# Four banks for scores, three for turned probabilities, and the mixings of a group begun in the third slot of a step

## The chip, the cores and the metric

The kernel runs on one core of one Trainium2 chip. Its metric is the device time of one launch in microseconds (us). TensorE (PE in the profile) multiplies and turns tiles into the eight banks of PSUM; VectorE (DVE), ScalarE (ACT) and GpSimd (POOL) do the rest; SyncE (SP) issues most DMAs.

## What is computed

One step of a two-layer network over 1024 latent tokens and 128 prompt tokens. Each layer normalises its input, multiplies it by one wide weight matrix, and feeds three branches (a Fourier mixing, a pooling and an attention with eight heads). The change touches the attention, which is in the reference

```python
def one(qblk):
    s = jnp.einsum('bqhd,bkhd->bhqk', qblk, k, preferred_element_type=jnp.float32) * scale
    p = jax.nn.softmax(s, axis=-1).astype(v.dtype)
    return jnp.einsum('bhqk,bkhd->bqhd', p, v)
```

with 8 heads, keys of 96 numbers and values of 64. The 1024 latent queries attend to 1024 latent keys and 128 cached ones; the 128 prompt queries attend to their own 128 keys.

## The kernel before

**Tiles.** The queries of a head are nine tiles of 128 rows. Tiles 0 to 7 are latent: their 1152 keys make three score parts of 384 columns. Tile 8 is the prompt: one part of 128 columns. Over the head's nine tiles that is 25 parts, and 200 in a layer.

**Stages of a tile.** TensorE computes a score part in three passes (`scores`, L1778, passes at L1607 to L1609) into a bank. VectorE takes its row maxima (L1450) and, after the last part, the negated maximum (L1456). ScalarE reads the bank once more and writes the exponentials to SBUF (`exps`, L832, with a short instruction that reads the accumulated row sum); that gives the score bank back. TensorE turns the 128-column blocks of the exponentials (`turn`, L1798) into another bank; with the last part it also turns the inverse row sum (L1802), for which it waits for VectorE (L1469, L1474). ScalarE copies the turned part out (`turned_high`, L848, and L855 for the sums), VectorE subtracts for the low half (L1463), which gives that bank back. Two tiles make a group; TensorE multiplies the nine key tiles of a group by the values (`mix`, two passes a key tile, L1823 and L1824) in one accumulation in the one bank of the mixed outputs. ScalarE lifts half of it (L867), VectorE adds (L1484), which gives the mixed bank back.

**Steps.** The engines each run the same loop over steps s, one per tile, with h, j = divmod(s, 9): h is the head, j the place in it. In step s TensorE turns tile s-1, scores tile s+1 and mixes a piece of a group; at the step's end it may compute a piece of the next head's queries or keys (`beside_pe`, L1736). ScalarE copies out the parts of tile s-1 alternately with the exponentials of tile s: the copy of part 0, the exponentials of part 0, and so on; a piece of the next head's queries stands between the exponentials of part 0 and the copy of part 1. The order in TensorE's step is a table:

```python
PE_STEP = (("turn", 0), ("score", 0), ("mix", 0), ("turn", 1), ("score", 1), ("mix", 1),
           ("turn", 2), ("score", 2), ("mix", 2))
```

`mix_slots` (L203) says which key tiles of which group stand in the three mix slots of a step. A group's mixing begins in a step with odd j (3, 5, 7, or 0 of the next head) and ends in the step after it.

**Banks.** `bank_plan` (L108) gives each kind of item a range of banks. The items of a kind use its banks in turn. Before it writes an item, TensorE waits in `pe_takes` (L417) until the item that had the bank before was read out: with five banks score part n waits for the exponentials of part n-5. Kind "attn" holds the turned parts and the pieces of the next head, in program order; "score" the score parts; "mixed" the mixings; "chan" six items of the Fourier branch just ahead of the attention.

Of the kernel before, what the change touches and what calls it, by code (L numbers as in the profile page):

```python
# [30 lines left out]
TT = TOK // P  # L31
# [4 lines left out]
HEADS = 8  # L36
# [71 lines left out]
def bank_plan():  # L108

    phases = []  # L110
    def add(layer, name, first, banks, count):
        phases.append(((layer, name), first, banks, count))
    add(0, "vec", 6, 1, 1)
    add(0, "mod", 0, 6, 16)
    add(0, "modt", 6, 1, 1)
    add(0, "norm", 6, 2, NCH * KF)
    for l in range(DEPTH):
        add(l, "tok", 0, 3, 2 * TT)
        add(l, "feat", 0, 6, 3 * len(FEAT_COLS))
        add(l, "turn", 0, 6, 14)  # L120
        add(l, "pool", 6, 2, 6)
        add(l, "val", 6, 2, KS)
        add(l, "seq", 6, 2, 12)
        add(l, "chan", 0, 6, 6)
        add(l, "attn", 6, 2, len(attention_items()))
        add(l, "score", 0, 5, HEADS * (3 * TT - 2))
        add(l, "mixed", 5, 1, HEADS * GROUPS)
        add(l, "gate", 0, 3, 3 * 3 * KF)
        add(l, "branch", 3, 3, 3 * 3 * KF)
        if l == 0:  # L130
            add(l, "later", 6, 2, later(GATE_ROWS)[0])
        add(l, "gbc", 6, 2, 4)
        if l == 0:
            add(l, "last", 6, 2, len(LATER) - later(GATE_ROWS)[0])
        add(l, "out", 0, 6, 3 * TT)
        if l + 1 < DEPTH:
            add(l + 1, "norm", 6, 2, NCH * KF)
    used = [0] * 8
    plan = {}
    for key, first, banks, count in phases:  # L140
        plan[key] = (first, banks, [used[first + i] for i in range(banks)])
        for i in range(banks):
            used[first + i] += len(range(i, count, banks))
    return plan
# [19 lines left out]
def later(u):  # L164

    units = 3 * KF - 2
    return range(len(LATER) * min(u, units) // units, len(LATER) * min(u + 1, units) // units)
# [9 lines left out]
GROUPS = 5  # L177
# [3 lines left out]
def parts(m):  # L181

    return 1 if m % TT == 8 else 3
# [19 lines left out]
def mix_slots(s):  # L203

    slots = [None, None, None]
    h, j = divmod(s, TT)
    if j in (3, 5, 7) and h < HEADS:
        slots[1], slots[2] = (h, (j - 3) // 2, (0, 1)), (h, (j - 3) // 2, (2, 3, 4))
    if j in (4, 6, 8) and h < HEADS:
        slots = [(h, (j - 4) // 2, (5,)), (h, (j - 4) // 2, (6, 7)), (h, (j - 4) // 2, (8,))]  # L210
    if h and j == 0:
        slots[1], slots[2] = (h - 1, 3, (0, 1)), (h - 1, 3, (2, 3, 4))
    if h and j == 1:
        slots = [(h - 1, 3, (5,)), (h - 1, 3, (6, 7)), (h - 1, 3, (8,))]
    if h and j == 2:
        slots[1] = (h - 1, 4, (0,))
    return slots


# [18 lines left out]
def mixed_in(s):  # L238

    for slot in mix_slots(s):  # L240
        if slot and (slot[2][-1] == 8 or slot[1] == 4):
            return slot[:2]
    return None


def beside(s):

    h, j = divmod(s, TT)
    if j in BESIDE_STEPS and h + 1 < HEADS:
        n = BESIDE_STEPS.index(j)  # L250
        return [("qk"[n // 3], h + 1, n % 3)]
    return []


def attention_items():

    order = [(kind, 0, i) for kind in "kq" for i in range(3)]
    for s in range(STEPS):
        if 1 <= s <= TILES:
            order += [("t", s - 1, g) for g in range(parts(s - 1))]  # L260
        order += beside(s)
    return {key: n for n, key in enumerate(order)}


def hybrid_step(nc, x_prompt, x_sample, cache_ckv, cache_krope, c, c_ctx, norm_g, w_mod, b_mod, w_in,
                pool_w, pool_scale, q_norm_g, w_q_up, kv_norm_g, w_kv_up, w_br_a, w_br_b, w_br_c,
                w_out, final_norm_g, tab, y_prompt, y_sample, new_ckv, new_krope, park_hi, park_lo, rows_mid):
    plan = bank_plan()


# [1331 lines left out]
    def _(pe):  # L1602
# [47 lines left out]
        for l in range(DEPTH):  # L1650
# [201 lines left out]
            for s in range(STEPS):  # L1852
                if s > TILES:
                    gate_high(s - TILES)
                for what, c in PE_STEP:
                    if s == TILES and (what, c) == ("mix", 1):
                        gate_high(0)
                    if what == "score" and s + 1 < TILES and c < parts(s + 1):
                        scores(s + 1, c)
                    if what == "turn" and turned(s - 1, c) is not None:  # L1860
                        turn(s - 1, turned(s - 1, c))
                    if what == "mix" and mix_slots(s)[c]:
                        mix(*mix_slots(s)[c])
                for it in beside(s):
                    beside_pe(*it)
# [88 lines left out]
```

## Time and profile before

| | us |
|---|---|
| median of 3 runs | 2224.97 |
| lowest and highest | 2221.03, 2226.98 |
| the profiled execution | 2222.64 |
| span of its trace | 2220.4 |
| the two attention loops in it | 304 to 621.4 and 1386 to 1703.5 |

The profiled execution took 2.2 us more than its span: that much lies around the first and the last instruction. A page row gives an engine's busy time and its share of the span. In the listing of waits a row says which engine and line waited for which, the total, the number of waits and the longest. In a timeline row stand the start, the duration, the engine, the line, the operation with output and input, and in brackets the idle time just ahead of it with what ended it.

### The profile page before, as it was taken

The page shows a single profiled execution, that of the slowest core. Times are in us where ns is not written, and L with a number is a line of the kernel's source. Part 1 is how long each engine was busy: PE and PEld are TensorE (multiplying, and loading weights), DVE is VectorE, ACT ScalarE, POOL GpSimd, SP SyncE. Part 2 cuts the span into 40 slices and gives each one's busy share as a digit, 9 for nine tenths or more (in the row PEclk, how much of TensorE's full clock was granted, in tenths as well). Part 3 has the DMA queues.
Part 4 walks back from the last instruction along what each step waited for, and adds up shares of the span by engine and source line. Part 5 has one row for each costly group of instructions (what it writes and reads, how often), then busy time and mean ns, then how long its engine had stood idle before and what let it go on. Part 6 is the DMA issues. An engine that isn't in the chain of part 4 may idle for free.

```text
span 2220.4 us, 35875 instructions
## 1 busy us (share of the span) xinstructions
PE 2131.5 (96%) x13185; PEld 2035.3 (92%) x13185; DVE 1090.4 (49%) x2823; ACT 886.7 (40%) x2223; POOL 653.6 (29%) x560
## 2 busy tenths in 40 slices
PE   7999999999999999999999999999999999999997
PEld 5899878888899999999989997888888999999997
DVE  2441268888864667663162314888886111120213
ACT  2521267777831212113152214777777112111312
POOL 1323122322322234333441311222323223343342
PEclk8999999999999999999999999999999999999999
DMA  9811000000343333224255100000005111111232
GB/s 275 267 33 31 26 1 1 1 1 1 121 155 85 95 83 100 78 63 143 74 197 163 40 1 26 1 2 1 1 14 192 48 36 48 40 46 39 65 124 85
DMA packets 194622, 155.67 MB, mean 70 GB/s; under 512 B 8637, under 2 KB 186001, under 8 KB 193425
## 3 DMA queue, kind: packets, MB, share of 16 engines
q1 hardware_dynamic: 194448, 153.38, 22.2%
q8 instruction: 106, 1.74, 0.3%
q14 instruction: 68, 0.55, 0.1%
HBM read 124.89 MB, written 28.48 MB: 69 GB/s over the span
## 4 chain that ended last, share of the span: by engine, by line
PE 84%; DVE 7%; ACT 4%; issue 3%; DMA 1%; POOL 0%; SPq 0%; DVEq 0%; POOLq 0%; ACTq 0%
PE ps L1607 23%; PE ps L1609 23%; PE ps L1608 23%; PE ps L1798 5%; PE ps L1823 3%; PE ps L1824 2%; DVE partmax L1450 1%; DVE probsT L1463 1%; PE ps L1617 1%; DVE kT L1420 1%; ACT kT L879 1%; PE ps L1841 1%; ACT probsT L848 1%; DVE xn_high L1201 1%; ACT probs L832 1%
## 5 line engine op out<-in xcount | busy, mean ns | idle before, releaser
L1607 PE MATMUL ps<-xn_high,split_br 128*128 128x384 f32 x1584 | 531.8, 336 | 0.0
L1609 PE MATMUL ps<-xn_high,split_br 128*128 128x384 f32 x1584 | 529.5, 334 | 0.0
L1608 PE MATMUL ps<-xn_low,split_br 128*128 128x384 f32 x1584 | 529.3, 334 | 0.0
L960 ACT ACTIVATE sigmoids<-ps 128x384 f32<-128x384 f32 x144 | 70.4, 492 | 613.5 <-PE ps L1609 613.5
L1608 PEld LDWEIGHTS ps<-xn_low,split_br 128*128 128x128 f32 x1584 | 297.5, 188 | 0.0
L1607 PEld LDWEIGHTS ps<-xn_high,split_br 128*128 128x128 f32 x1584 | 297.4, 188 | 0.0
L1609 PEld LDWEIGHTS ps<-xn_high,split_br 128*128 128x128 f32 x1584 | 297.3, 188 | 0.0
L1002 POOL TENSOR_TENSOR split_br<-raw,split_br 128x1024 fp32r<-128x1024 f32 x82 | 198.2, 2418 | 320.4 <-ACT split_br L693 320.4
L1463 DVE TENSOR_TENSOR probsT<-ps,probsT 128x384 fp32r<-128x384 f32 x384 | 213.1, 555 | 70.1 <-ACT sum_inv_rows L855 42.7
L832 ACT ACTIVATE probs<-ps,negmax 128x384 f32<-128x384 f32 (+1 forms) x400 | 229.1, 573 | 29.3 <-DVE negmax L1456 28.7
L1798 PE MATMUL ps<-ident,probs 128*128 128x128 f32 x1168 | 197.5, 276 | 31.0 <-DVE kT L1420 15.8
L848 ACT ACTIVATE probsT<-ps 128x384 fp32r<-128x384 f32 x384 | 188.6, 491 | 79.9 <-PE ps L1798 46.7
L1450 DVE TENSOR_REDUCE partmax<-ps 128x1 f32<-128x384 f32 (+1 forms) x400 | 212.1, 534 | 2.0 <-PE ps L1609 1.8
L1541 DVE TENSOR_TENSOR products<-ps,sigmoids 128x384 f32<-128x384 f32 x96 | 53.5, 557 | 293.0 <-PE ps L1609 240.3
L1798 PEld LDWEIGHTS ps<-ident,probs 128*128 128x128 f32 x1168 | 132.0, 140 | 70.6 <-issue 65.3
L1136 POOL TENSOR_TENSOR merged<-merged,products 128x384 f32<-128x384 f32 x90 | 92.2, 1025 | 334.7 <-DVE products L1541 333.8
L1607 PE MATMUL ps<-split_br,xn_high 128*128 128x256 f32 (+1 forms) x576 | 182.2, 316 | 5.3 <-DVE xn_low L1204 5.0
L1609 PE MATMUL ps<-split_br,xn_low 128*128 128x256 f32 (+1 forms) x576 | 178.7, 310 | 0.0
L1608 PE MATMUL ps<-split_br,xn_high 128*128 128x256 f32 (+1 forms) x576 | 178.7, 310 | 0.0
L1823 PE MATMUL ps<-probsT,head_values 128*128 128x256 f32 x576 | 156.3, 291 | 12.0 <-DVE mixed_out L1484 12.0
L1607 PE MATMUL ps<-kT,qT 128*128 128x384 f32 (+1 forms) x400 | 163.3, 408 | 1.6 <-ACT probs L832 1.0
L1091 POOL TENSOR_TENSOR branch<-mixed_out,branch 64x256 f32<-64x256 f32 (+1 forms) x80 | 54.2, 678 | 335.3 <-DVE mixed_out L1484 334.4
(227 smaller groups left out, 4197.4 us busy)
## 6 DMA issues: line engine op xcount, KB each, us to landing
raw<-in_w_in SPq DMA_DIRECT2D x74, 512.0 KB, 3.9
raw<-in_w_mod SPq DMA_DIRECT2D x48, 512.0 KB, 5.0
park_high<-xn_high SPq DMA_DIRECT2D x6, 1536.0 KB, 6.4
park_low<-xn_low SPq DMA_DIRECT2D x6, 1536.0 KB, 10.6
xn_high<-park_high SPq DMA_DIRECT2D x2, 4608.0 KB, 16.0
rows<-in_x_sample SPq DMA_DIRECT2D x16, 512.0 KB, 6.8
raw<-in_w_out SPq DMA_DIRECT2D x16, 512.0 KB, 6.5
rows_mid<-rows SPq DMA_DIRECT2D x9, 512.0 KB, 2.6
```

The lines of the kernel that those rows point to most:

```text
L832: a.activation((P0, P1)[m % 2][:, c * CH:c * CH + w], PS[:, b, 0:w], ACT.Exp, bias=negmax[:, m % 2:m % 2 + 1], accum_out=partsum[:, m % 2, ...
L848: ins = a.activation(turned_place(m, gg, 0), PS[:, b, 0:n * P].rearrange("p (k c) -> p k c", k=n), ACT.Copy)
L960: a.activation(sig[:, ch, :], PS[:, b, 0:CH], ACT.Sigmoid).then_inc(bank_free[b], 1)
L1002: g.tensor_tensor(d[:, 1], raw_unit(n), d[:, 0].bitcast(F32), ALU.subtract).then_inc(S("split_low"), 1)
L1136: g.tensor_tensor(Y[:, u % KF, sl], Y[:, u % KF, sl], prod[:, q % 2, :], ALU.add).then_inc(S("y_sum"), 1)
L1450: v.tensor_reduce(partmax[:, m % 2, c:c + 1], PS[:, b, 0:w], AX.X, ALU.max).then_inc(S("partmax"), 1)
L1463: v.tensor_tensor(turned_place(m, gg, 1), PS[:, b, 0:n * P].rearrange("p (k c) -> p k c", k=n), turned_place(m, gg, 0).bitcast(F32), ALU.s ...
L1607: mm(out, wh, xh, start=first, stop=False)
L1608: mm(out, wh, xl, start=False, stop=False)
L1609: return mm(out, wl, xh, start=False, stop=last)
L1798: ins = nc.tensor.transpose(PS[:, b, q * P:(q + 1) * P], (P0, P1)[m % 2][:, (3 * gg + q) * P:(3 * gg + q + 1) * P], ident[:])
L1823: mm(PS[:, b, 0:w], vhl, xh, start=(kt == 0 or gr == 4), stop=False)
```

## The change

The banks of the attention's kinds are cut otherwise: "score" has four banks in place of five (0 to 3), "mixed" moves from bank 5 to bank 4, "attn" has three in place of two (5 to 7), and "chan" loses its sixth bank. And where a group's mixing began with two key tiles in the second slot and went on with three in the third, it now begins with five in the third. The steps in which a mixing ends keep their slots (one, two and one key tiles). The prompt tile's mixing moves from the second slot of its step to the third.

```diff
-        add(l, "chan", 0, 6, 6)
-        add(l, "attn", 6, 2, len(attention_items()))
-        add(l, "score", 0, 5, HEADS * (3 * TT - 2))
-        add(l, "mixed", 5, 1, HEADS * GROUPS)
+        add(l, "chan", 0, 5, 6)
+        add(l, "attn", 5, 3, len(attention_items()))
+        add(l, "score", 0, 4, HEADS * (3 * TT - 2))
+        add(l, "mixed", 4, 1, HEADS * GROUPS)
...
     if j in (3, 5, 7) and h < HEADS:
-        slots[1], slots[2] = (h, (j - 3) // 2, (0, 1)), (h, (j - 3) // 2, (2, 3, 4))
+        slots[2] = (h, (j - 3) // 2, (0, 1, 2, 3, 4))
...
     if h and j == 0:
-        slots[1], slots[2] = (h - 1, 3, (0, 1)), (h - 1, 3, (2, 3, 4))
+        slots[2] = (h - 1, 3, (0, 1, 2, 3, 4))
...
     if h and j == 2:
-        slots[1] = (h - 1, 4, (0,))
+        slots[2] = (h - 1, 4, (0,))
```

The instructions of VectorE, ScalarE, GpSimd and SyncE keep their order. TensorE's change at two places; in the brackets stand the semaphores that an instruction waits for, and bank_free with a number means that this bank must have been read out.

The first place is TensorE from the second turned part of a step with odd j to the third score part (step j = 3 of head 0). Before:

```order
L1798 MATMUL ps<-ident,probs_94 128x128 x2
L1607 MATMUL ps<-kT,qT 128x384 [waits bank_free3]
L1608 MATMUL ps<-kT,qT 128x384
L1609 MATMUL ps<-kT,qT 128x384
L1823 MATMUL ps<-probsT,head_values 128x256 [waits bank_free6,v_ready,bank_free5]
L1824 MATMUL ps<-probsT,head_values 128x256
L1823 MATMUL ps<-probsT,head_values 128x256
L1824 MATMUL ps<-probsT,head_values 128x256
L1798 MATMUL ps<-ident,probs_94 128x128 [waits bank_free6,bank_free3]
L1798 MATMUL ps<-ident,probs_94 128x128 x2
L1802 MATMUL ps<-ident,sum_inv 128x128 [waits sum_inv]
L1607 MATMUL ps<-kT,qT 128x384 [waits bank_free4]
```

Of the change:

```order
L1798 MATMUL ps<-ident,probs_94 128x128 x2
L1607 MATMUL ps<-kT,qT 128x384 [waits bank_free1]
L1608 MATMUL ps<-kT,qT 128x384
L1609 MATMUL ps<-kT,qT 128x384
L1798 MATMUL ps<-ident,probs_94 128x128 [waits bank_free6,bank_free0]
L1798 MATMUL ps<-ident,probs_94 128x128 x2
L1802 MATMUL ps<-ident,sum_inv 128x128 [waits sum_inv]
L1607 MATMUL ps<-kT,qT 128x384 [waits bank_free2]
L1608 MATMUL ps<-kT,qT 128x384
L1609 MATMUL ps<-kT,qT 128x384
L1823 MATMUL ps<-probsT,head_values 128x256 [waits bank_free5,bank_free6,v_ready,bank_free4]
L1824 MATMUL ps<-probsT,head_values 128x256
```

The four matmuls of two key tiles no longer stand between the second score part and the third turned part.

The second place is TensorE where one head passes into the next (step j = 0), from its first score part on; that step has two score parts before its one turned part. Before:

```order
L1607 MATMUL ps<-kT,qT 128x384 [waits bank_free4]
L1608 MATMUL ps<-kT,qT 128x384
L1609 MATMUL ps<-kT,qT 128x384
L1823 MATMUL ps<-probsT,head_values 128x256 [waits bank_free7,bank_free6,bank_free5]
L1824 MATMUL ps<-probsT,head_values 128x256
L1823 MATMUL ps<-probsT,head_values 128x256
L1824 MATMUL ps<-probsT,head_values 128x256
L1798 MATMUL ps<-ident,probs_94 128x128 [waits bank_free6,bank_free4]
L1802 MATMUL ps<-ident,sum_inv 128x128 [waits sum_inv]
L1607 MATMUL ps<-kT,qT 128x384 [waits bank_free0]
```

Of the change:

```order
L1607 MATMUL ps<-kT,qT 128x384 [waits bank_free1]
L1608 MATMUL ps<-kT,qT 128x384
L1609 MATMUL ps<-kT,qT 128x384
L1798 MATMUL ps<-ident,probs_94 128x128 [waits bank_free5,bank_free0]
L1802 MATMUL ps<-ident,sum_inv 128x128 [waits sum_inv]
L1607 MATMUL ps<-kT,qT 128x384 [waits bank_free2]
L1608 MATMUL ps<-kT,qT 128x384
L1609 MATMUL ps<-kT,qT 128x384
L1823 MATMUL ps<-probsT,head_values 128x256 [waits bank_free5,bank_free4]
L1824 MATMUL ps<-probsT,head_values 128x256
```

The mixing, with its wait for the mixed bank, has moved behind the turned part and the third score part.

## Rows read from the trace of the kernel before

**Rows 1.** Page, part 1: busy time, share of the span, instructions.

```profile
PE 2131.5 (96%) x13185; PEld 2035.3 (92%) x13185; DVE 1090.4 (49%) x2823; ACT 886.7 (40%) x2223; POOL 653.6 (29%) x560
```

**Rows 2.** Windows of both attention loops: length, busy time by engine, PEclk, DMA share, GB/s.

```profile
304.00:621.40 317.40, 295.12 (x2014) 267.98 (x2013) 264.38 (x751) 252.12 (x758) 90.11 (x107) 1.00 0.08 28
1386.00:1703.50 317.50, 294.91 (x2012) 267.79 (x2011) 263.94 (x751) 251.78 (x758) 89.80 (x106) 1.00 0.08 28
```

**Rows 3.** Listing of waits of the whole trace, TensorE's in the attention.

```profile
PE ps L1798 <- DVE kT L1420: 15.8, 42, 0.5
...
PE ps L1798 <- DVE probsT L1463: 12.5, 34, 0.7
PE ps L1823 <- DVE mixed_out L1484: 12.0, 20, 0.7
```

**Rows 4.** Timeline, start of the first loop: an exponential, and TensorE waiting for it.

```profile
305.86 0.58 ACT L832 ACTIVATE probs<-ps,negmax 128x384 f32<-128x384 f32 x1 [0.19 <-DVE negmax L1456]
...
306.59 0.45 PE L1607 MATMUL ps<-kT,qT 128*128 128x384 f32 x1 [0.50 <-ACT probs L832]
```

**Rows 5.** Timeline of TensorE, step j = 3 of head 3 and the next step's first row.

```profile
437.30 0.52 PE L1798 MATMUL ps<-ident,probs 128*128 128x128 f32 x3
...
438.72 0.42 PE L1607 MATMUL ps<-kT,qT 128*128 128x384 f32 x1
...
440.16 0.42 PE L1607 MATMUL ps<-kT,qT 128*128 128x384 f32 x1
...
441.48 0.34 PE L1607 MATMUL ps<-qhatT,wq_head 128*128 128x384 f32 x1
...
442.53 0.27 PE L1798 MATMUL ps<-ident,probs 128*128 128x128 f32 x1
```

**Rows 6.** Timeline of ScalarE, the same step: exponentials of parts 0 and 1.

```profile
438.25 0.57 ACT L832 ACTIVATE probs<-ps,negmax 128x384 f32<-128x384 f32 x1
...
439.59 0.59 ACT L832 ACTIVATE probs<-ps,negmax 128x384 f32<-128x384 f32 x1
```

**Rows 7.** Timeline, step j = 4: exponentials of part 0, second score part, next step.

```profile
443.44 0.58 ACT L832 ACTIVATE probs<-ps,negmax 128x384 f32<-128x384 f32 x1
...
443.86 0.42 PE L1607 MATMUL ps<-kT,qT 128*128 128x384 f32 x1
...
447.05 0.52 PE L1798 MATMUL ps<-ident,probs 128*128 128x128 f32 x3
```

**Rows 8.** Timeline, steps j = 5 and 6 and the first row of j = 7.

```profile
448.45 0.57 ACT L832 ACTIVATE probs<-ps,negmax 128x384 f32<-128x384 f32 x1
...
452.30 0.49 PE L1798 MATMUL ps<-ident,probs 128*128 128x128 f32 x3
...
453.36 0.57 ACT L832 ACTIVATE probs<-ps,negmax 128x384 f32<-128x384 f32 x1
...
454.02 0.52 PE L1798 MATMUL ps<-ident,probs 128*128 128x128 f32 x3 [0.47 <-DVE kT L1420]
...
457.49 0.52 PE L1798 MATMUL ps<-ident,probs 128*128 128x128 f32 x3 [0.38 <-DVE probsT L1463]
```

**Rows 9.** Timeline, step j = 7: VectorE's inverse sum, its turning, the next step.

```profile
459.49 0.16 DVE L1474 RECIPROCAL sum_inv<-rowsum 128x1 f32<-128x1 f32 x1
...
459.89 0.27 PE L1802 MATMUL ps<-ident,sum_inv 128*128 128x128 f32 x1
...
460.71 0.49 PE L1798 MATMUL ps<-ident,probs 128*128 128x128 f32 x3
```

**Rows 10.** Timeline, from head 3 into head 4 (j = 0), up to j = 1.

```profile
465.51 0.33 PE L1607 MATMUL ps<-kT,qT 128*128 128x384 f32 x1
...
466.42 0.58 ACT L832 ACTIVATE probs<-ps,negmax 128x384 f32<-128x384 f32 x1 [0.86 <-DVE negmax L1456]
...
466.90 0.39 PE L1823 MATMUL ps<-probsT,head_values 128*128 128x256 f32 x1 [0.71 <-DVE mixed_out L1484]
...
468.94 0.49 PE L1798 MATMUL ps<-ident,probs 128*128 128x128 f32 x3
```

## The prediction, made before the result

> **What bounds the kernel now.** I read the page first: TensorE is busy for 96% of the span, VectorE for 49% [rows 1]. That is a mean over stages, so the windows of the two attention loops come next, since the change touches little else: of 317.4 and 317.5 us TensorE is busy for 295.1 and 294.9, VectorE for 264 and ScalarE for 252, at full clock [rows 2]. TensorE sets the pace there too, with 44.9 us without work. The listing of waits says what that is [rows 3]: 28.3 us ahead of turned parts (L1798), which wait for VectorE to empty an "attn" bank (15.8 and 12.5 us), and 12.0 us ahead of mixings, which wait for VectorE to empty the mixed bank. These 40.3 us are all that the change can remove.
>
> **What one wait for a score bank looks like.** It happens once in a loop before. At 305.86 the exponentials of part 0 of tile 0 begin, and TensorE, which waits for that bank, goes on at 306.59 [rows 4]. So a score part can be written from 0.73 us after the start of the exponentials that give its bank back. I use this E + 0.73 throughout; it is one case, the same in both loops.
>
> **What four banks ask for.** In step s TensorE scores tile s+1. With five banks its second part needs the exponentials of tile s-1's last part, done in the step before. With four, part n needs n-4: the second part needs the exponentials of part 0 of tile s, the third those of part 1 of tile s. ScalarE makes these in the same step, and its order is unchanged: the exponentials of part 0 stand behind the copy of the turned part 0 of the same step. They cannot start earlier than the step allows, so TensorE's own step start sets a floor under its second score part.
>
> Issue costs of TensorE by differences of rows: a piece of queries takes 1.05 (441.48 to 442.53); third score part and three key tiles take 1.32 (440.16 to 441.48); second score part, two key tiles and the turned part with its sum take 1.44 (438.72 to 440.16) [rows 5]. With 0.24 for a key tile that makes 0.61 for a score part and 0.36 for the turned part with its sum; one without is 0.25. A piece of keys is three passes, 0.70, and 0.35 for the short last one.
>
> **Step j = 3**, times from its start at 437.30. Exponentials of part 0 start at 0.95, of part 1 at 2.29 [rows 6]. Before, the second score part starts at 1.42, the third at 2.86, the step ends at 5.23 [rows 5]. With the change the second waits until 0.95 + 0.73 = 1.68. The turned part follows at 2.29 and ends at 2.65, but the third score part needs 2.29 + 0.73 = 3.02. It ends at 3.63, then five key tiles (1.18) and the queries (1.05): 5.86. The step becomes 0.63 longer. Of this 0.47 is the two key tiles that before stood where TensorE now waits: the move takes away the very work that would cover the wait.
>
> **Step j = 4.** Exponentials at 0.91, second score part at 1.33 before [rows 5, 7], at 1.64 after: +0.31. The third needs nothing more, since two key tiles still lie between. At the end the next turned part waited about 0.2 for its bank before (the step lasts 4.52, its work 4.33); three banks remove that. Net +0.11.
>
> **Step j = 5.** Exponentials at 1.40 before [rows 7, 8], late because ScalarE first copies the piece of keys; that piece ends 0.2 later against the step's start, so 1.59. Second score part at 2.32, turned part, third at about 3.37 (bank of part 1), five key tiles, keys: 5.87 against 5.25: +0.62, although the wait for the keys' bank is gone.
>
> **Step j = 6** gains. Before it lasts 5.19, with a wait for an attn bank ahead of the second turned part and one of 0.38 behind the step [rows 8]; its work alone is 3.98. The exponentials start at 1.06 [rows 8], so the second score part waits until 1.79 in place of 1.34: 4.43, or -0.76.
>
> **Step j = 7** has one short score part. Before, two key tiles stand ahead of the third turned part, whose sum (VectorE, ready at 459.65) is turned at 459.89; the step lasts 3.22 [rows 8, 9]. After, nothing stands there: TensorE is at the sum some 1.1 us after the start and waits for VectorE, whose chain comes only 0.2 earlier on the clock while the step starts 0.76 earlier; the sum is turned at about 2.8, then five key tiles: 4.06, +0.84.
>
> **Head to head (j = 8 and 0).** From 460.71 to the next j = 1 are 8.23 us [rows 9, 10]. The second score part of j = 0 starts at 465.51 before; with four banks it needs exponentials that start at 466.42 because VectorE's maximum is late. VectorE's chain is 0.3 us earlier against the step's start after the change, so the part starts at about 6.1 rather than 4.80; before, TensorE then idled up to 466.90 for the mixed bank [rows 10], a wait that vanishes. From 6.1: score 0.61, turned part 0.24, score 0.61, five key tiles 1.18: 8.75, +0.52.
>
> **Steps j = 1 and 2** have the patterns of 4 and 3. I take +0.30 for j = 1 (the 0.31 of j = 4; no bank wait behind it) and +0.60 for j = 2 (near the 0.63 of j = 3; its one small mixing moves too, but its third part waits longer).
>
> **Sum.** 0.30 + 0.60 + 0.63 + 0.11 + 0.62 - 0.76 + 0.84 + 0.52 = 2.86 us a head, 16 heads: 45.8. Head 0 has no early mixings and comes out lower, head 7 has no pieces of a next head to lean on and comes out higher; I let them cancel. Start of a loop: the second score part of tile 1 now waits for the first exponentials instead of the third, about +0.5, less 0.3 for the third piece of keys just ahead, which no longer waits for a bank: +0.4 for two layers. "chan" with five banks: its sixth item takes the bank of its first, read long before, 0. Total +46 us. Against the profiled execution, 2222.6, this is 2269; that execution lies 2.3 below the median, well inside the runs' own spread, and I leave the figure there: 2269.
>
> **Bounds.** Low end: if only the waits of second score parts count and the third parts find their banks, j = 2, 3 and 5 fall to some 0.3 each and j = 7 to 0.3: about 1.0 a head, +16, 2239. High end: the gain of step 6 does not come, because ScalarE and VectorE are the ones who are late by then (+12), and ScalarE's lag in j = 5 carries on (+0.5 a head, +8): 2289.
>
> **Rivals.**
>
> A, faster: the removed waits decide. If the exponentials come earlier once the third score part stands ahead of the mixing, because their maximum is ready sooner, the floor falls away and the 40.3 us of [rows 3] go: 2182. It decides where exponentials of part 0 start less than about 0.6 us after the step; in the rows they start at 0.91 to 1.40, behind the copy of the turned part, not behind the maximum. Against it also [rows 7]: in j = 4 nothing waited, and 1.33 is still short of 1.64.
>
> The Trainium skill, page "Perfetto Trace Analysis", section "Optimization Strategy", says that a gap repeating on the engine that should be saturated can mean that there is not enough PSUM for the next tile; it speaks for a third bank ahead of L1798 and would give this rival's 2182 if the bank came free of charge. The rows show such gaps [rows 3, 8], but the bank is taken from scores, whose margin is negative.
>
> B, no change: new waits equal old ones, as where ScalarE's idle time lets it pull ahead by half of what is asked. Per head 2.5 us of old waits would have to be met by 2.5 of new: 2219 to 2231.
>
> C, slower but milder, second parts alone: 2231 to 2248, as in the low bound.
>
> D, worse: over 2292. ScalarE and VectorE, late in one step, push the next one's start; all terms as computed and +1.5 a head on top: 2293.
>
> **How the numbers follow.** Forecast (2248 to 2292) 0.66, A 0.07, B 0.05, C 0.15, D 0.07. A measurement of this kernel can tell about 0.3% from no change. A is faster, B the same, the rest slower: 0.07, 0.05, 0.88. The range from 2238 to 2292 leaves out A, B, D and a part of C, together just under 0.2 with half of C inside.
>
> **What would show it.** In the trace after: the waits of L1798 for VectorE (28.3 us) and of L1823 for the mixed bank (12.0) nearly gone; in their place TensorE's L1607 in the attention waiting for ScalarE's L832, some 60 to 80 us in about 150 waits and more, and L1802 for L1474 in step j = 7; loops of about 340 us in place of 317.4; the time outside them unchanged. Step j = 3 near 5.9 us and step j = 6 near 4.4. I am wrong if L832 starts less than 0.9 after the step, if a bank is free sooner than 0.73 after that, or if the loops are no longer.

## The result: 46.6 us slower, and the profile after

| | before | after |
|---|---|---|
| median of the runs shown, us | 2223.46 (4 runs) | 2270.05 (4 runs) |
| lowest and highest | 2221.03, 2226.98 | 2268.28, 2271.30 |
| span of the profiled execution | 2220.4 | 2269.1 |

The ratio is 1.0209, with a 95% interval of 1.0196 to 1.0223. The forecast was 2269, and its range 2238 to 2292.

The page answers [rows 1] with the same instructions and a lower share for TensorE. The second row is its chain of work that ended last; before, TensorE had 84% of that chain, VectorE 7% and ScalarE 4%.

```profile
PE 2142.5 (94%) x13185; PEld 2041.6 (90%) x13185; DVE 1092.5 (48%) x2823; ACT 886.1 (39%) x2223; POOL 652.6 (29%) x560
...
PE 79%; ACT 9%; DVE 6%; issue 5%; DMA 1%; POOL 0%; SPq 0%; DVEq 0%; ACTq 0%; POOLq 0%
```

The windows of the two attention loops answer [rows 2]. They are cut here from the first score part to the end of the last mixing; cut in that way, the loops before last 318.2 and 318.7 us with TensorE busy for 296.0 and 296.1.

```profile
302.10:643.40 341.30, 301.78 (x2016) 271.99 (x2017) 265.40 (x752) 252.06 (x758) 90.48 (x107) 1.00 0.07 26
1410.60:1752.20 341.60, 301.88 (x2016) 271.97 (x2017) 265.21 (x752) 252.10 (x758) 90.45 (x107) 1.00 0.07 26
```

Each loop is 23 us longer: +23.1 and +22.9. VectorE and ScalarE do the same work in it. Between the loops the trace is 3.7 us longer, ahead of them 1.1 us shorter, and behind them the same. So the traces differ by 48.7 us, of which 46.0 lie where the prediction put them.

The listing of waits answers [rows 3], and the page's groups give the same lines with their releasers.

```profile
PEld ps L1607 <- ACT probs L832: 99.7, 144, 1.9
...
PE ps L1607 <- ACT probs L832: 60.3, 88, 1.6
...
PE ps L1802 <- DVE sum_inv L1474: 9.4, 16, 0.8
```

```profile
L1607 PE MATMUL ps<-kT,qT 128*128 128x384 f32 (+1 forms) x400 | 168.0, 420 | 65.9 <-ACT probs L832 60.3
...
L1798 PE MATMUL ps<-ident,probs 128*128 128x128 f32 x1168 | 192.9, 273 | 4.1 <-DVE kT L1420 4.1
```

The waits of the turned parts fell from 28.3 us to 4.1, and those for the mixed bank from 12.0 to nothing that the listing shows. In their place stand 60.3 us of score parts (L1607) that wait for exponentials (L832).

TensorE's idle time in the loops grew by 34.3 us (44.9 to 79.2) and the loops by 46.0. The other 11.7 us appear as busy time, 603.7 in place of 592.0 us, although the instructions are the same. The rows of matmuls overlap. A score pass has a row of 0.34 us, but the next one starts 0.17 or 0.18 later, and busy time counts the overlap once. Where TensorE then waits, the row is counted whole. A score pass that starts behind a wait has a longer row besides (440 ns on the mean, against 411 without a wait), so the mean of the first score pass is 420 ns, against 408 before. The Trainium skill ("Perfetto Trace Analysis", section "Identifying the Most-Contended Engine") says that the busy share of matmuls is no good measure of how close a kernel is to TensorE's peak, since pipelined instructions look smaller in a trace. This trace agrees, as these 11.7 us show. **Loss is read from the length of a step, not from idle time alone.**

Step j = 3 of head 3 starts at 445.61 and answers [rows 5] and [rows 6]. The rows are TensorE's and ScalarE's timelines in order of time.

```profile
445.61 0.49 PE L1798 MATMUL ps<-ident,probs 128*128 128x128 f32 x3
...
446.47 0.49 PE L1798 MATMUL ps<-ident,probs 128*128 128x128 f32 x3
...
446.52 0.57 ACT L832 ACTIVATE probs<-ps,negmax 128x384 f32<-128x384 f32 x1
...
447.24 0.44 PE L1607 MATMUL ps<-kT,qT 128*128 128x384 f32 x1 [0.28 <-ACT probs L832]
...
447.86 0.59 ACT L832 ACTIVATE probs<-ps,negmax 128x384 f32<-128x384 f32 x1
...
448.20 0.27 PE L1802 MATMUL ps<-ident,sum_inv 128*128 128x128 f32 x1
...
448.60 0.44 PE L1607 MATMUL ps<-kT,qT 128*128 128x384 f32 x1
...
451.46 0.49 PE L1798 MATMUL ps<-ident,probs 128*128 128x128 f32 x3
```

The exponentials of part 0 start at 446.52 and the second score part at 447.24, 0.72 later. Those of part 1 start at 447.86 and the third score part at 448.60, 0.74 later. The step lasts 5.85 us; 5.86 was forecast. The bracket says 0.28, but the second score part starts 0.77 after the turned part ahead of it (446.47), where a score part that waits for nothing starts 0.24 or 0.25 behind one. The third score part shows no bracket at all: the row of the sum just ahead, which ends at 448.47, fills most of the gap on paper.

### The profile page after: what moved, and what is told of

Same layout as the page of the kernel before. It is cut to its first block, busy times and chain, and to the rows that moved or that the text cites. A ratio compares the mean times of both kernels' runs of the same rounds, so it can differ in the third digit from the quotient of the medians.

```text
span 2269.1 us, 35875 instructions
## 1 busy us (share of the span) xinstructions
PE 2142.5 (94%) x13185; PEld 2041.6 (90%) x13185; DVE 1092.5 (48%) x2823; ACT 886.1 (39%) x2223; POOL 652.6 (29%) x560
## 4 chain that ended last, share of the span: by engine, by line
PE 79%; ACT 9%; DVE 6%; issue 5%; DMA 1%; POOL 0%; SPq 0%; DVEq 0%; ACTq 0%; POOLq 0%
PE ps L1607 24%; PE ps L1609 22%; PE ps L1608 22%; ACT probs L832 4%; ACT probsT L848 2%; PE ps L1824 2%; PE ps L1823 2%; PE ps L1798 2%; DVE probsT L1463 1%; DVE partmax L1450 1%; PE ps L1617 1%; DMA raw<-in_w_mod 1%; PE ps L1841 1%; DVE xn_high L1201 1%; PE ps L1802 1%
## 5 line engine op out<-in xcount | busy, mean ns | idle before, releaser
L1607 PE MATMUL ps<-xn_high,split_br 128*128 128x384 f32 x1584 | 532.3, 336 | 0.0
L1607 PEld LDWEIGHTS ps<-xn_high,split_br 128*128 128x128 f32 x1584 | 297.9, 188 | 0.0
L832 ACT ACTIVATE probs<-ps,negmax 128x384 f32<-128x384 f32 (+1 forms) x400 | 229.6, 574 | 25.2 <-DVE negmax L1456 25.2
L1607 PE MATMUL ps<-kT,qT 128*128 128x384 f32 (+1 forms) x400 | 168.0, 420 | 65.9 <-ACT probs L832 60.3
L1798 PE MATMUL ps<-ident,probs 128*128 128x128 f32 x1168 | 192.9, 273 | 4.1 <-DVE kT L1420 4.1
L1607 PE MATMUL ps<-split_br,xn_high 128*128 128x256 f32 (+1 forms) x576 | 182.0, 316 | 5.3 <-DVE xn_low L1204 5.0
L1607 PEld LDWEIGHTS ps<-kT,qT 128*128 128x128 f32 x400 | 75.7, 189 | 104.6 <-ACT probs L832 99.7
L1798 PEld LDWEIGHTS ps<-ident,probs 128*128 128x128 f32 x1168 | 142.7, 140 | 17.6 <-issue 7.1
```

What stands on the lines that cost most here:

```text
L832: a.activation((P0, P1)[m % 2][:, c * CH:c * CH + w], PS[:, b, 0:w], ACT.Exp, bias=negmax[:, m % 2:m % 2 + 1], accum_out=partsum[:, m % 2, ...
L1607: mm(out, wh, xh, start=first, stop=False)
L1798: ins = nc.tensor.transpose(PS[:, b, q * P:(q + 1) * P], (P0, P1)[m % 2][:, (3 * gg + q) * P:(3 * gg + q + 1) * P], ident[:])
```

## The experiments

All times are medians, and each ratio is against the kernel before on the same chip. Its medians were 2221.61 (7 runs) for the first four kernels, 2222.43 (12 runs) for the next four, 2222.5 (7) for e9 to e11 and 2222.56 (7) for e12.

My theory was that the score bank sets the loss: a score part cannot start before the exponentials four parts earlier have started, plus 0.73 us. The rival theories were that the moved mixings cost it, that VectorE's chain does, or that ScalarE's order does.

### The two halves apart: e1 and e2

e1 is the change without its new mixing places:

```diff
-        slots[2] = (h, (j - 3) // 2, (0, 1, 2, 3, 4))
+        slots[1], slots[2] = (h, (j - 3) // 2, (0, 1)), (h, (j - 3) // 2, (2, 3, 4))
...
-        slots[2] = (h - 1, 3, (0, 1, 2, 3, 4))
+        slots[1], slots[2] = (h - 1, 3, (0, 1)), (h - 1, 3, (2, 3, 4))
...
-        slots[2] = (h - 1, 4, (0,))
+        slots[1] = (h - 1, 4, (0,))
```

> Only the banks are cut as in the change (score 4, attn 3, mixed 1); the mix slots stay as before (two key tiles in the second slot, three in the third). Theory (a score part waits until 0.73 us after the start of the exponentials four parts back; the moved key tiles uncover that wait): the second score part waits as in the change, but the two key tiles then stand ahead of the third score part, which finds its bank free, and ahead of the sum in step j = 7. Against the change that gives back 0.37 in step j = 3, 0.2 in j = 2, 0.1 in j = 5, 0.5 in j = 7, so about 1.1 us a head, 18 us: about 2252. Rival (the late mixing costs nothing by itself, the banks alone make the whole loss): 2270.

Measured: 2260.67 us, ratio 1.0179 (1.0164 to 1.0194).

e2 is the kernel before with the new mixing places, so the same lines the other way round.

> Only the mix slots are moved as in the change; banks as before (score 5, attn 2, mixed 1). Theory: no score part waits for exponentials of its own step, so the move costs only where the sum of step j = 7 is not ready (about +0.3 a head) and 0.1 in j = 5, and gives back what TensorE waited for the mixed bank in head 7: 2223 to 2232. Rival (the move is what costs, since five key tiles in one block starve VectorE and ScalarE): 2245 or more.

Measured: 2229.53 us, ratio 1.0038 (1.0023 to 1.0053). e2's waits:

```profile
PE ps L1798 <- DVE probsT L1463: 23.0, 44, 1.4
PE ps L1798 <- DVE kT L1420: 15.8, 42, 0.5
PE ps L1802 <- DVE sum_inv L1474: 11.8, 14, 1.0
```

The banks alone cost 39 us and the places alone 8; together they make 47, and the change cost 46.6. **The banks are five sixths of it.** e1 came out 9 us over what I expected. Its steps j = 3 and 7 gained what the rows promised (0.39 and 0.48 us against the whole change), but the passage from head to head lost 0.5 us that I had not foreseen, since the mixing's wait for its bank returns there (8.9 us in the listing of e1).

The two halves add up in the sum, but not step by step. Over the first 70 steps of the first loop e1 is 18.3 us longer than before, e2 4.1 and the change 22.7. Steps j = 2 and 3 lose 9.9 us in the change against 6.8 in e1 and e2 together: there the moved mixings uncover the wait, as the prediction said. In the other steps the change loses 2.8 us less than the two together. e2's largest loss is 3.8 us in step j = 7, and it is not a wait for the inverse sum, as I had expected. TensorE waits there for VectorE to empty a turned bank:

```profile
459.19 0.52 PE L1798 MATMUL ps<-ident,probs 128*128 128x128 f32 x3 [0.53 <-DVE probsT L1463]
```

Of the 23.0 us of this wait 14.1 stand in j = 7 (5.7 before), while the 11.8 us for the sum all stand between two heads.

### One bank at a time: e3 and e11

e3 gives the third turned bank back, and keeps four for scores. The bank so freed lies unused.

```diff
-        add(l, "attn", 5, 3, len(attention_items()))
+        add(l, "attn", 6, 2, len(attention_items()))
```

> The change with the third attn bank taken back (score 4, attn 2, mixed 1, one bank unused). Tells what the third attn bank was worth. Theory: it is worth most in step j = 6 (where the change gained 0.75 us) and the 0.2 us ahead of j = 5; without it about 0.9 us a head come back as waits of L1798 for VectorE, 14 us: about 2284. Rival (the third attn bank is worth nothing once the score banks set the pace): 2270.

Measured: 2274.68 us, ratio 1.0239 (1.0221 to 1.0256). Its waits:

```profile
PE ps L1607 <- ACT probs L832: 38.2, 52, 1.5
PE ps L1798 <- DVE kT L1420: 15.9, 42, 0.5
PE ps L1798 <- DVE probsT L1463: 14.3, 32, 1.0
```

e3 differs from e2 by the fifth score bank (and by the mixed bank's number and the sixth bank of "chan"): 2229.5 against 2274.7, so that one bank is worth 45 us. The third turned bank, all that the change buys with it, is worth 4.6 (2274.7 to 2270.1), or 6.5 if each kernel is taken against the kernel before on its own chip. I had expected 14. The bank takes 26 us of waits of turned parts away, and 22 us more of waits for exponentials come back. Step by step, over the first loop, it takes 5.2 us out of j = 6, as the prediction said, but j = 7, which begins earlier by it, gives 2.5 of them back. With two turned banks TensorE waits there for a bank, with three for the inverse sum.

e11 takes one more score bank away, and that one lies unused too.

```diff
-        add(l, "score", 0, 4, HEADS * (3 * TT - 2))
+        add(l, "score", 0, 3, HEADS * (3 * TT - 2))
```

> The change with three banks for scores in place of four; the bank so freed lies unused. Nothing of the output changes. Theory: with n banks a score part waits for the exponentials of the part n before it. With five that is two parts of the step before, with four one part of the step before, with three it is the same part's of the step before, so that every part of every step waits and TensorE can work ahead of ScalarE by no more than the matmuls between two score parts. A step with five key tiles then comes to about 9 us in place of 5.9, and the kernel to 2600 to 2700 us. Rival: banks of scores cost a like amount each (45 us from five to four): 2310 to 2320 us.

Measured: 2874.23 us, one run. Its waits, then both engines' timelines over two score parts:

```profile
PE ps L1607 <- ACT probs L832: 431.4, 334, 2.1
```

```profile
363.17 0.58 ACT L832 ACTIVATE probs<-ps,negmax 128x384 f32<-128x384 f32 x1
...
363.89 0.45 PE L1607 MATMUL ps<-kT,qT 128*128 128x384 f32 x1 [1.14 <-ACT probs L832]
...
366.17 0.58 ACT L832 ACTIVATE probs<-ps,negmax 128x384 f32<-128x384 f32 x1
...
366.90 0.44 PE L1607 MATMUL ps<-kT,qT 128*128 128x384 f32 x1 [1.31 <-ACT probs L832]
```

The listing has 334 waits for 400 score parts, where the change had 88, and both parts here start 0.72 and 0.73 us behind the start of the exponentials that they wait for. With three banks a score part waits for the exponentials of the same part one tile back, which ScalarE makes in the same step. This is the plainest proof of the mechanism: five to four banks costs 45 us, four to three 604. The 604 are not waits alone. The granted clock was 0.89 over the whole span (0.994 in the change), and 0.79 between 300 and 700 us; what that cost was not separated. So the 9 us that I had expected for a step with five key tiles became 12.1 in j = 3, and 2600 to 2700 us was missed.

### Where the floor can be lowered: e4

In e4 ScalarE makes the exponentials of a part ahead of the copy of the turned part, to start them sooner.

```diff
-                    if turned(s - 1, c) is not None:
-                        turned_high(s - 1, turned(s - 1, c))
                     if s < TILES and c < parts(s):
                         exps(s, c)
+                    if turned(s - 1, c) is not None:
+                        turned_high(s - 1, turned(s - 1, c))
```

> The change, and ScalarE's order in a step turned round: the exponentials of part c of tile s ahead of the copy of the turned part c of tile s-1. Banks and TensorE's order as in the change. Theory (the floor under the second score part is the copy that stands ahead of the exponentials): exponentials of part 0 start 0.4 to 0.9 us earlier, TensorE's waits for them (60 us ahead of L1607) shrink by more than half; the copy comes later, so the sum in odd steps comes later too: about -1.8 us a head, 2241 (2232 to 2256). Rival (the floor is VectorE's maximum): no change, 2270.

Measured: 2269.29 us, ratio 1.0215 (1.0200 to 1.0231). I expected 2241 and was wrong; it can't be told from the change. Its waits, then the timeline of its step j = 3, which starts at 446.44:

```profile
PE ps L1607 <- ACT probs L832: 42.4, 52, 1.6
PE ps L1802 <- DVE sum_inv L1474: 38.0, 77, 2.1
```

```profile
447.31 0.58 ACT L832 ACTIVATE probs<-ps,negmax 128x384 f32<-128x384 f32 x1 [1.05 <-DVE negmax L1456]
...
448.03 0.44 PE L1607 MATMUL ps<-kT,qT 128*128 128x384 f32 x1 [0.24 <-ACT probs L832]
```

Two things took the gain. In j = 3 the exponentials start only 0.87 after the step, against 0.91, since they now wait for VectorE's negated maximum, as the rival said. Where they did start sooner (j = 1, 2, 4, 6: each 0.3 to 0.5 shorter), VectorE gets its turned part later, and behind it stands the sum, for which TensorE waits 38.0 us in place of 9.4. Steps j = 7 and 8 grew by 0.4 and 1.1 us. The rule of 0.72 held here too (447.31 to 448.03).

### VectorE's order and the weights: e5 to e8

e5 is the change with VectorE's sum ahead of its first low half, against the waits of L1802:

```diff
-DVE_STEP = (("beside", 0), ("unmix", 0), ("low", 0), ("sum", 0), ("max", 0), ("low", 1),
+DVE_STEP = (("beside", 0), ("unmix", 0), ("sum", 0), ("low", 0), ("max", 0), ("low", 1),
```

> The change, and VectorE makes the inverse sum of tile s-1 ahead of its low half of part 0, not behind it. In step j = 7 TensorE then finds the sum about 1.4 us earlier. Theory (the pass from head to head is set by VectorE: the exponentials of part 0 in step j = 0 start when its chain of maxima is through): the step j = 7 gets shorter by 0.5 to 1.3 us, and steps j = 8 and 0 together longer by nearly as much, so the time moves by at most 0.3 us a head: 2264 to 2271. Rival (the sum is a cost of its own, 0.84 a head as in the prediction's term): 2257.

Measured: 2275.58 us, ratio 1.0241 (1.0223 to 1.0259). That is 4.6 above my range. Step j = 7 fell from 4.13 to 3.66 as wanted, but j = 0, counted here from its turned part, rose from 1.93 to 3.47. The last section shows why.

e6 is the change, and e7 the kernel before, with VectorE's splitting of the query weights of a later head moved from step j = 7 into j = 1 and 3 (the other line, `head_weights_low`, stands behind the second condition):

```diff
-                if j == 7 and h + 2 < HEADS:
+                if j == 1 and h + 2 < HEADS:
...
+                if j == 3 and h + 2 < HEADS:
```

> The change, and VectorE's 1.1 us of query weights for the head after next, made at the end of step j = 7, are made earlier: the high halves at the end of j = 1, the low halves at the end of j = 3, where the rows show VectorE idle ahead of its next wait. Theory: the chain of VectorE that ends in the exponentials of j = 0 is up to 1.1 us earlier in six heads of each layer; about 0.7 of that a head becomes time, 8 us: 2262 (2258 to 2267). Rival (the score banks alone set the pass): 2270.

> The kernel before, with the same move of the query weights. In head 6 of the trace before, which has none to make, step j = 8 lasts 6.0 us in place of 6.65 to 6.78. Theory: 0.7 us in each of twelve heads, 8 us off: 2214 (2211 to 2219). Rival (the weights only move VectorE's delay into steps 2 and 4): 2222.

Measured: e6 2267.55, ratio 1.0201 (1.0183 to 1.0220); e7 2220.02, ratio 0.9990 (0.9981 to 1.0000). I expected 2262 and 2214. e6 can't be told from the change, nor e7 from the kernel before, so the rivals (2270 and 2222) came nearer both times. In e7 steps j = 8 and 0 gain 3.8 us over the first loop, and j = 2, 4 and 7 give back 2.8 (1.4, 1.0, 0.4). VectorE has as little room there.

e8 puts e2, e5's order and e7's places together.

> Banks as before (score 5, attn 2), the mix slots of the change, the sum ahead of the low half, and the query weights early. Slots alone came to 8 us above the kernel before, with 0.5 us a head lost in j = 7 to the wait for the sum. Theory: the sum first gives that back and the weights some 0.7 a head more, because without the wait for the mixed bank TensorE is held in j = 0 only by the exponentials: 2212 (2205 to 2220). Rival (a wait for the attn banks takes the place of each): 2225 to 2230.

Measured: 2246.75 us, ratio 1.0110 (1.0094 to 1.0126), above both what I and the rival expected. Its waits of L1799 (L1798 in the kernel before; one line more stands ahead of it):

```profile
PE ps L1799 <- DVE probsT L1463: 32.9, 55, 1.7
```

The theory rested on a wrong reading of e2: it says that e2 loses 0.5 us a head in j = 7 to the wait for the sum, but e2 waits there for a turned bank. With two banks for turned parts, a low half made later is a bank given back later, and the waits for it in j = 7 rose from 14.1 to 18.4 us. The waits for the sum, between the heads, stayed at 11.7. In j = 2 come 5.5 us of waits behind VectorE's piece of queries (L1416), which e7 has too. The sum's place and the weights' place were not tried apart here, so what each has of the 17 us over e2 stays open.

### Covering the wait: e9, e10 and e12

e9 starts from e1 (the banks alone) and moves the next head's piece, which needs no exponentials, from the step's end to behind the first score part. ScalarE's and VectorE's share of it moves into the same step, and its place in the rotation of the turned banks with it; TensorE's lines are shown.

```diff
                     if what == "mix" and mix_slots(s)[c]:
                         mix(*mix_slots(s)[c])
-                for it in beside(s):
-                    beside_pe(*it)
+                    if (what, c) == ("score", 0):
+                        for it in beside(s):
+                            beside_pe(*it)
```

> The bank counts of the change (four banks for scores, three for turned probabilities, one mixed), the mixings in before's places, and one move more: the next head's piece, which TensorE makes at the step's end, is made right behind the step's first score part, and ScalarE and VectorE take it out early in the same step. Theory: the loss of the change comes from TensorE waiting for exponentials (60.3 us of waits at L1607), and it can be covered by work that needs no exponentials; the piece is such work, 0.8 to 0.9 us in each step that has one. Worked out step by step from the rows of head 3: j=3 some 5.1 us (5.46 with the banks alone), j=4 4.4, j=5 4.7 to 4.9 (5.79), j=6 4.0 to 4.2 (4.44); j=7 and the head pass stay as with the banks alone. That is 1.2 us a head under before, some 17 us over both loops: 2203 us (2195 to 2222), below both kernels. Rival: the third score part now stands behind the exponentials of the first part and the copies of VectorE get late, so that the wait only moves: 2235 to 2250 us.

Measured: 2239.87 us, ratio 1.0077 (1.0062 to 1.0092). That is 20.8 us less than e1, and 37 more than I expected; the rival's range (2235 to 2250) held it. The waits, and the rows where step j = 2 begins at 434.38 (L1604 is L1607 of the other kernels):

```profile
PE ps L1604 <- ACT probs L832: 45.4, 66, 1.6
```

```profile
434.36 0.58 ACT L832 ACTIVATE probs<-ps,negmax 128x384 f32<-128x384 f32 x1
...
435.18 0.41 PE L1604 MATMUL ps<-kT,qT 128*128 128x384 f32 x1 [0.30 <-ACT probs L832]
```

Steps j = 5 and 6 did what was expected (4.67 and 4.06 us against 5.79 and 4.44). In j = 2 and 3 the wait moved from the second score part to the first: that one needs the last exponentials of the tile before, and these now start only as the step begins, 0.82 ahead of the part. Over the first 70 steps of the first loop, j = 5 and 6 gain 10.5 us against e1 and j = 1 gains 2.0, while j = 3 and 4 lose 3.9 again. Of these, 1.6 are in head 7, where TensorE waits 0.45 and 1.19 us in one step and the granted clock then falls (0.61 from 606.0 to 609.7).

e10 is the whole change with the same move.

> The whole change, its places of the mixings too, with the next head's piece right behind the step's first score part, as in the run beside it. Theory that the piece covers the wait for exponentials: 0.5 to 0.8 us a head more than the run beside it, 2210 to 2225 us, 45 to 60 us under the change. Rival that the wait only moves: 2245 to 2260 us.

Measured: 2250.31 us, ratio 1.0125 (1.0108 to 1.0142), 19.7 less than the change. The rival's range held it.

e12 is e9 with the third exponentials of a step ahead of the third copy (except in j = 7).

```diff
+                    ahead = c == 2 and s % TT != 7
+                    if ahead and s < TILES and c < parts(s):
+                        exps(s, c)
                     if turned(s - 1, c) is not None:
                         turned_high(s - 1, turned(s - 1, c))
-                    if s < TILES and c < parts(s):
+                    if not ahead and s < TILES and c < parts(s):
                         exps(s, c)
```

> The bank counts of the change, the mixings in before's places, the next head's piece right behind the first score part (the run e9), and one move more: in each step but j=7 ScalarE makes the third part's exponentials ahead of the third turned part's copy, not behind it. In e9 the wait did not go altogether: in j=2 and j=3 the step's first score part begins at 0.80 and 0.89 us after the step's start, where it would begin at 0.25 without a wait, since the third part's exponentials of the step before end 0.65 to 0.7 us into the step. Theory: they then end before the step begins; j=2 falls from 4.70 to about 4.15 and j=3 from 5.56 to about 4.9, some 1.2 us a head over 14 passes, 17 us: 2223 us (2214 to 2232), level with the kernel before or just under it. Rival: the copy comes 0.6 us later, VectorE's low half and its maxima after it, and the wait comes back behind VectorE, which has 4.4 to 4.8 us of work in such a step: 2234 to 2245 us.

Measured: 2245.69 us, ratio 1.0105 (1.0088 to 1.0122), 5.8 more than e9. Its step j = 2 starts at 436.63:

```profile
437.31 0.56 DVE L1462 TENSOR_TENSOR probsT<-ps,probsT 128x384 fp32r<-128x384 f32 x1 [1.06 <-ACT sum_inv_rows L855]
...
438.36 0.16 DVE L1455 TENSOR_REDUCE negmax<-partmax 128x1 f32<-128x3 f32 x1
...
438.55 0.58 ACT L832 ACTIVATE probs<-ps,negmax 128x384 f32<-128x384 f32 x1 [0.43 <-DVE negmax L1455]
...
439.28 0.44 PE L1607 MATMUL ps<-kT,qT 128*128 128x384 f32 x1 [0.24 <-ACT probs L832]
```

The first score part no longer waits, and the step is 0.26 shorter. But VectorE stood idle for 1.06 us until the late copy was there. Its maximum came late, so did the next exponentials (1.92 into the step, against 1.47 in e9), and the second score part waited for them, again 0.73 behind their start. In this head j = 3 and 5 are 0.4 longer and j = 7 is 0.2 longer. Over the first loop j = 5 and 7 lose 3.7 us against e9 and j = 2 gains 1.5; in j = 3 the loss of heads 0 to 6 (1.9) is made good in head 7, where the clock no longer falls. TensorE's waits for the mixed bank, which VectorE empties, rose from 4.0 to 14.0 us. The rival's range ended 0.7 us below the measured time, but its mechanism is the one seen: with four banks TensorE, ScalarE and VectorE form one ring, and in e4, e5 and e12 the new order of one let another come last.

No kernel with four score banks reached the kernel before. The best of all twelve is e7, which can't be told from it.

## Why the prediction was right

The lengths of the steps of head 3 in us, j = 1 to 8 and j = 0 of head 4, from one trace of each kernel:

| | j=1 | 2 | 3 | 4 | 5 | 6 | 7 | 8 and 0 |
|---|---|---|---|---|---|---|---|---|
| before | 4.67 | 4.28 | 5.23 | 4.52 | 5.25 | 5.19 | 3.22 | 8.23 |
| after | 5.01 | 4.91 | 5.85 | 4.63 | 5.79 | 4.43 | 4.13 | 8.49 |
| difference | +0.34 | +0.63 | +0.62 | +0.11 | +0.54 | -0.76 | +0.91 | +0.26 |
| predicted | +0.30 | +0.60 | +0.63 | +0.11 | +0.62 | -0.76 | +0.84 | +0.52 |

**The floor of E + 0.73** was taken from one wait at the loop's start [rows 4]. It is no single case: over both loops of the change 112 of 126 second score parts start 0.71 or 0.72 after the start of their exponentials. No score part of the change starts sooner, and none in any of the fourteen traces sooner than 0.70. A few first score parts that wait start 0.82 after, as in e9 above, four of them in the change; what adds 0.1 there stays open.

**Steps j = 1 to 6** came out within 0.08 us each. That j = 4 loses least and j = 6 gains is as worked out: one has two key tiles left in the second slot, the other had the waits that the third bank removes.

**Step j = 7** waits for VectorE's inverse sum, as forecast. The timeline answers [rows 9]; the step starts at 466.31 and the next at 470.44.

```profile
468.85 0.16 DVE L1474 RECIPROCAL sum_inv<-rowsum 128x1 f32<-128x1 f32 x1
...
469.07 0.32 PE L1802 MATMUL ps<-ident,sum_inv 128*128 128x128 f32 x1 [0.70 <-DVE sum_inv L1474]
```

The sum is turned 2.76 after the step's start, where 2.8 stood in the prediction.

**From head to head** the loss was mis-sized: +0.26 to +0.29 behind heads 1, 3 and 5 and +0.39 to +0.42 behind heads 0, 2 and 4, against +0.52 (behind head 6 it was +0.9). The mechanism is there, as the answer to [rows 10] shows:

```profile
475.63 0.58 ACT L832 ACTIVATE probs<-ps,negmax 128x384 f32<-128x384 f32 x1 [0.98 <-DVE negmax L1456]
...
476.35 0.44 PE L1607 MATMUL ps<-kT,qT 128*128 128x384 f32 x1 [1.59 <-ACT probs L832]
```

The part starts 5.91 after the start of j = 8, not 6.1, since VectorE's maximum came 0.5 earlier against the step's start, not 0.3.

**The sum.** 2.86 us a head times eight makes 22.9 a loop, and the loops grew by 23.1 and 22.9. From the first turned part over 70 steps the difference is 22.7 in the first loop and 22.6 in the second. That it fits is in part luck. Heads 1 to 5 came to 2.63 to 2.75 each, not 2.86. Head 0 came to 2.5, head 6 to 3.2, and head 7 to 3.5 without its last step, since its j = 6 gains nothing (+0.32): I had let heads 0 and 7 cancel without working, and the two late heads made up for what the others fell short. The start of a loop (from its first score part to its first turned part) cost 0.58, near the +0.5, without the 0.3 that I took off for the piece of keys.

**The rivals.** A (the removed waits decide) fell: they were removed, 28.3 and 12.0 us to 4.1 and 0, and the kernel is slower. The Trainium skill's rule on consistent bubbles ("Perfetto Trace Analysis", "Optimization Strategy") points at a real shortage here, since the third bank does remove that gap. e3 shows what the rule leaves open: the bank is worth 4.6 us where it goes and 45 where it comes from. B fell because new waits were larger than old ones. C (second score parts alone) fell because third parts waited as well: step j = 3 would have grown by 0.3, and grew by 0.62. D fell because no delay added up: j = 4 and 6 came out as worked out.

**Beside the sum.** The forecast of about 150 waits is true for the weight loads (144) but not for the matmuls (88). Of the 3.7 us between the loops nothing was forecast; the last section shows them. Two sums of the prediction don't come out, and neither touches the forecast. The terms of the low end (0.3 each for j = 1, 2, 3, 5 and 7, the others as they stand) make 1.37 us a head and 2245, not 1.0 and 2239. And what the range leaves out has a chance of 0.27 with half of C inside, not just under 0.2. A forecast of 46 met 46.6 because such terms are small, not because each was right.

## What to carry to other kernels

Before a bank of PSUM is taken from a rotation, write down for each item of that rotation which read gives its bank back with one bank less, when that read starts in the same step, and what TensorE could do until then. Here that floor cost 45 us, seven to ten times what the same bank brought elsewhere. And where work is moved, ask whether it is the work that covers the wait: with five score banks the move of the mixings cost 8 us, and pulling forward a piece that waits for nothing gave 20 back. But in a ring of three engines the gain of one link is mostly passed to the next.

## What the runs showed of the hardware

**The clock fell behind most waits that were only a little longer.** The wait from head to head was expected to cost its own length. In the change TensorE idles 1.48 to 1.60 us there by the brackets, 14 times, and the clock stays at 1.00 behind each. In e5 it idles 1.84 us between heads 3 and 4. The windows of e5 around it:

```profile
476.50:478.40 1.90, 0.09 (x1) 0.00 (x0) 1.77 (x7) 0.69 (x3) 0.12 (x1) 1.00 0.00 0
478.40:482.50 4.10, 4.07 (x18) 3.98 (x19) 2.47 (x8) 1.55 (x6) 0.61 (x1) 0.58 0.01 2
```

```profile
478.43 0.45 PE L1607 MATMUL ps<-kT,qT 128*128 128x384 f32 x1 [1.84 <-ACT probs L832]
```

The granted clock is 0.58 over the 4.1 us behind the wait, most of them at 1.2 GHz in place of 2.4. Step j = 0 becomes 1.5 us longer than in the change. But a wait of the same length between heads 1 and 2 leaves the clock alone:

```profile
390.37 0.44 PE L1607 MATMUL ps<-kT,qT 128*128 128x384 f32 x1 [1.84 <-ACT probs L832]
...
390.37:394.47 4.10, 4.10 (x29) 3.88 (x29) 2.74 (x9) 2.52 (x9) 0.57 (x1) 1.00 0.00 0
```

Eleven of e5's passes from head to head idle 1.84 to 2.08 us. The clock falls behind eight of them (0.58 to 0.64 over 4.1 us) and stays at 1.00 behind three, two of 1.84 and one of 2.08. So the length of the wait alone does not decide it, and what does stays open. Steps j = 8 and 0 of e5 are 7.7 and 7.9 us longer over the two loops, j = 7 is 3.7 shorter in each. That is why e5 is slower.

**One slow VectorE instruction between the loops.** Most of the 3.7 us are in one place of the profiled execution after, where TensorE waits for the sums of the modulation:

```profile
659.27 6.32 DVE L1231 SCALAR_TENSOR_TENSOR mod_sums<-raw,silu_c,mod_sums 128x128 f32<-128x128 f32 x14
...
665.74 0.41 PE L1625 MATMUL ps<-ident,mod_sums 128*128 128x128 f32 x2 [3.20 <-DVE mod_sums L1231]
```

```profile
665.90:668.00 2.10, 2.10 (x11) 2.10 (x11) 2.07 (x8) 0.00 (x0) 0.00 (x0) 0.69 0.68 191
668.00:670.00 2.00, 2.00 (x8) 2.00 (x7) 2.00 (x9) 0.00 (x0) 0.00 (x0) 0.50 0.41 121
```

Before, the same 14 instructions took 4.23 us and TensorE waited 1.12. Here one of them took 2.42 alone, the wait is 3.20, and the clock falls behind it as in e5. In e3's trace the same instruction, the 13th of the 14, also takes 2.42 us and TensorE waits 3.20; that execution is 6 us above e3's other three. The spans of the other three executions of the change are 2266.2, 2266.9 and 2268.9, so up to 2.9 us of it may come and go. What held that instruction up was not tried and stays open.
